# Query and gate projections of a decoder step as 2x2x2 Strassen products

## The reference

```python
# layer 0: HGRN2 mixer, then a ConvFFN; then ONE set of keys and values for layer 1
hn = rmsnorm(h, kv_norm)
k, v, fl = jnp.split(hn @ w_kvf, [D_MODEL, 2 * D_MODEL], axis=-1)
k = rmsnorm(k.reshape(B, T, FOX_HEADS, FOX_HEAD_DIM), k_norm)
logf = jax.nn.log_sigmoid((fl + b_f).astype(jnp.float32))
# layer 1: forgetting attention
hn = rmsnorm(h, norm_mix[layer])
qg = hn @ fox_w_qg[j]                                # 1024 -> 2048
q, gate = jnp.split(qg, 2, axis=-1)
q = rmsnorm(q.reshape(B, T, FOX_HEADS, FOX_HEAD_DIM), q_norm[j])
o = fox_attention(q, k, v, cumulative logf)          # prompt: causal; samples: 512 cached keys and values each
mix = (o.reshape(B, T, D_MODEL) * jax.nn.sigmoid(gate)) @ fox_w_o[j]
h = h + mix                                          # then a second ConvFFN
```

## Time and profile before

| | us |
|---|---|
| median of three runs | 1550.22 |
| lowest, highest | 1549.51, 1550.86 |
| the profiled execution | 1551.19 |
| its span | 1549.6 |
| PE busy in the span | 1524.7 (98%) |
| PE weight loads | 1447.2 (93%) |
| DVE, ACT, POOL busy | 955.0, 747.9, 455.9 |

### The profile page before, as it was taken

The page is one execution under the profiler, slowest core; times in us unless marked ns, Lnnn a source line. Parts: engine busy times, 40 slices in busy tenths (PEclk is TensorE's granted clock), DMA queues, the critical chain, the costliest instruction groups (busy, mean ns, idle before and its releaser), DMA issues. The chain is left out here.

```text
span 1549.6 us, 36591 instructions
## 1 busy us (share of the span) xinstructions
PE 1524.7 (98%) x13662; PEld 1447.2 (93%) x13662; DVE 955.0 (62%) x1699; ACT 747.9 (48%) x1283; POOL 455.9 (29%) x500
## 2 busy tenths in 40 slices
PE   7999999999999999999999999999999999999999
PEld 7999999989999999999999999755899999999999
DVE  5777777767877676533344444688539876767222
ACT  6444444435466566422344455666435565666111
POOL 1222222224575554000010000222126665551000
PEclk9999999999999999999999999999999999999999
DMA  6222222213132222223233334599422222213321
GB/s 217 69 86 93 91 85 78 78 69 113 61 126 91 95 94 92 81 76 89 89 126 116 128 97 150 182 345 367 142 87 82 100 91 94 95 62 118 104 90 46
DMA packets 53363, 174.22 MB, mean 112 GB/s; under 512 B 7298, under 2 KB 9746, under 8 KB 53250
## 3 DMA queue, kind: packets, MB, share of 16 engines
q1 hardware_dynamic: 48578, 156.43, 30.6%
q0 software_dynamic: 4672, 16.24, 2.9%
HBM read 160.07 MB, written 12.57 MB: 111 GB/s over the span
## 5 line engine op out<-in xcount | busy, mean ns | idle before, releaser
L545 ACT ACTIVATE w_hi<-w_raw 128x1024 fp32r<-128x1024 f32 (+1 forms) x143 | 146.9, 1027 | 304.5 <-PE acc L2073 268.6
L1048 DVE TENSOR_TENSOR w_lo<-w_raw,w_hi 128x1024 fp32r<-128x1024 f32 (+1 forms) x141 | 173.4, 1230 | 144.6 <-ACT w_hi L545 142.9
L2073 PE MATMUL acc<-xl,w_hi 128*128 128x288 f32 x1008 | 224.1, 304 | 8.8 <-DVE xl L1060 7.9
L2073 PE MATMUL acc<-xh,w_hi 128*128 128x288 f32 x1008 | 216.1, 296 | 0.0
L2073 PE MATMUL acc<-xh,w_lo 128*128 128x288 f32 x1008 | 215.8, 296 | 0.0
L2073 PEld LDWEIGHTS acc<-xl,w_hi 128*128 128x128 f32 x1008 | 160.9, 189 | 17.0 <-issue 13.2
L2266 PE MATMUL aux<-ffn_xsh,w_lo 128*128 128x288 f32 x576 | 169.9, 295 | 0.0
L2266 PE MATMUL aux<-ffn_xsh,w_hi 128*128 128x288 f32 x576 | 169.7, 295 | 0.0
L2266 PE MATMUL aux<-ffn_xsl,w_hi 128*128 128x288 f32 x576 | 169.3, 294 | 0.2
L2073 PEld LDWEIGHTS acc<-xh,w_hi 128*128 128x128 f32 x1008 | 162.5, 189 | 0.0
L2073 PEld LDWEIGHTS acc<-xh,w_lo 128*128 128x128 f32 x1008 | 162.4, 189 | 0.0
(11 more groups left out here) (347 smaller groups left out, 3445.1 us busy)
## 6 DMA issues: line engine op xcount, KB each, us to landing
w_raw<-w_fi_in SPq DMA_DIRECT2D x88, 512.0 KB, 3.7
w_raw<-w_fo_in SPq DMA_DIRECT2D x32, 512.0 KB, 3.5
att_Vd<-cache_v_in SPq DMA_DIRECT2D x32, 512.0 KB, 5.9
w_raw<-w_mix_in SPq DMA_DIRECT2D x31, 512.0 KB, 3.5
w_raw<-w_kv_in SPq DMA_DIRECT2D x16, 512.0 KB, 3.6
w_raw<-w_qg_in SPq DMA_DIRECT2D x16, 512.0 KB, 3.5
dec_Kd<-cache_k_in SPq DMA_DIRECT2D x16, 512.0 KB, 7.1
w_raw<-cache_k_in SPq DMA_DIRECT2D x16, 512.0 KB, 7.8
```

The lines of the kernel that those rows point to most:

```text
L545: nc.scalar.activation((w_hi[:, pos.slot % SPL] if dst is None else dst)[:, 0:width], w_raw[:, pos.slot, 0:width] if raw is None else raw[ ...
L1048: nc.vector.tensor_tensor(low[:, 0:width], w_raw[:, pos.slot, 0:width] if raw is None else raw[:], high[:, 0:width].bitcast(F32), ALU.subt ...
L2073: mm = nc.tensor.matmul(dst[:, hf, 0:HALF], W[:, 128 * (j0 + j):128 * (j0 + j) + 128], x[:, HALF * hf:HALF * hf + HALF], start=(first and ...
```

## The change

- Query block p and gate block p become one Strassen pair: seven products of 12 matmuls, `q_product`, six in `qg_pair(p)` and the seventh, `q_gate_first(p)`, in the next pair (for the last pair at its end).
- The token-side operands `q_xh`, `q_xl` (7 x 4 tiles of 288) take the place of `x2h`/`x2l`. They are made in KV pairs 2 to 5: `q_operand` (four DVE operations on `h`, now with `rms` and gain in them), `q_operand_sums` (four on POOL), `q_operand_hi` (one ACT copy of 2016 columns) and `q_operand_lo` (one DVE subtraction of 2016).
- The weight sums are made in QG by `q_sum`, `q_sum_hi`, `q_sum_lo`, `q_weight_diff`; the low part of the whole block (`q_block_lo`) and of a gate half (`q_gate_lo`) and the square of the query tile (`q_square`) go to POOL. The sigmoid's last exponential moves out of QG into `att(i)`.
- The sums need room: `h` is written to memory (`h_keep`, 2.36 MB) on SP's queue at the start of KV, ahead of the seven constants, and read back after the last cached values.
- The attention buffers lie elsewhere now, mostly on the operands: SP's `key_bias(0)`, `key_bias(1)`, `key_pages(0)` and `key_pages(1)` wait for products of the last QG pair.
- The key mean of pair 7 goes inside the last value block; the scan over the cached log-forget values is done before KV pair 7.

```diff
             sp.dma_start(pg[:], d["pages"]).then_inc(ld_table, 16)
+            sp.wait_ge(h_ok, 2 * DT)
+            sp.dma_start(d["h_keep"], h[:].rearrange("p m t -> p (m t)")).then_inc(w_half, 16)
             for dst, src in ((w_log[:], d["w_log"]), (group_sum[:], ...
...
-            sp.wait_ge(block_done, B_QG)
+            for p in range(2, DT):
+                for j in range(2):
+                    load(Pos(B_QG + 2 * p + j), d["w_qg"][2 * p + j], ready=(lo_done, B_QG + 2 * p - 2))
+            load(Pos(B_WO1), d["w_o1"][0], ready=(lo_done, B_QG + 14))
+            sp.wait_ge(c_dram, 16)
+            sp.wait_ge(grp_ps, 5 * (FAST + DT - 1) + 1)
             sp.dma_start(tri[:], d["att_masks"][:, 0:P]).then_inc(ld_mask, 16)
-            sp.wait_ge(c_dram, 16)
             key_bias(0, 0)
-            for j in range(4):
-                load(Pos(B_QG + 12 + j), d["w_qg"][12 + j])
+            sp.wait_ge(grp_ps, 5 * (FAST + DT - 1) + 2)
             key_bias(1, 1)
+            sp.wait_ge(grp_ps, 5 * (FAST + DT))
             key_pages(0)
-            load(Pos(B_WO1), d["w_o1"][0])
             key_pages(1)
             sp.wait_ge(block_done, B_WO1)
             sp.wait_ge(cs_dram, 32)
+            sp.wait_ge(km_ps, 16)
             sample_bias(0)
...
+            sp.dma_start(h[:].rearrange("p m t -> p (m t)"), d["h_keep"]).then_inc(w_half, 16)
             sp.wait_ge(d_ps, NSEQ)
...
+            def qg_pair(p):                       # TensorE
+                k, s, tile = p % 2, FAST + p, T_QG + 2 * p
+                x, y, z = [aux[:, b, 0:HALF] for b in (k, 2, 3)]
+                n = q_weight_n(p)
+                pe.wait_ge(lo_done, B_QG + 2 * p + 1)
+                if p == 0:
+                    pe.wait_ge(s_lo, q_part_n(4))
+                    pe.wait_ge(kln_ok, DT)
+                pe.wait_ge(evac, tile - 2)
+                q_product(x, 0, w_hi[:, 0, 0:512], w_lo[:, 0, 0:512], False).then_inc(grp_ps, 1)
+                if p == 0:
+                    last_turn_v()
+                    pe.wait_ge(vt_ok, 14)
+                pe.wait_ge(evac, tile - 1)
+                q_product(y, 1, w_hi[:, 0, 512:1024], w_lo[:, 0, 512:1024], False).then_inc(grp_ps, 1)
+                pe.wait_ge(s_lo, n + 1)
+                q_product(z, 2, q_wxh[:, 0], q_wxl[:, 0], False).then_inc(grp_ps, 1)
+                if p:
+                    if p == 1:
+                        pe.wait_ge(vt_ok, 16)
+                    key_mean(p + 7, acc[:, 1])
+                    q_gate_first(p - 1)
+                if p == DT - 1:
+                    pe.wait_ge(s_lo, n + 3)
+                    score(0, 0)
+                pe.wait_ge(s_lo, n + 2)
+                pe.wait_ge(snap_ok, 3 * s + 1)
+                q_product(x, 3, q_wxh[:, 1], q_wxl[:, 1], True).then_inc(grp_ps, 1)
+                pe.wait_ge(s_lo, n + 3)
+                pe.wait_ge(snap_ok, 3 * s + 2)
+                q_product(z, 4, w_hi[:, 1, 0:512], w_lo[:, 1, 0:512], True).then_inc(block_done, 1)
+                pe.wait_ge(s_lo, n + 4)
+                pe.wait_ge(snap_ok, 3 * s + 3)
+                q_product(x, 5, w_hi[:, 1, 512:1024], w_lo[:, 1, 512:1024], True).then_inc(grp_ps, 1)
+                if p == DT - 1:
+                    q_gate_first(p)
+                    key_mean(15, acc[:, 1])
...
+                if last:                          # DVE, end of its qg_pair(p)
+                    first_probs()
+                else:
+                    q_sum_lo(2, p + 1)
+                if p:
+                    gate_logsig(p - 1)
+                if last:
+                    gate_halves(p)
+                    square_lo(sqq, p + 8)
+                    gate_rest(p)
...
+            def kv_pair(p):                       # ACT
+                if p:
+                    hi(Pos(B_KV + 1 + 2 * p))
+                    if p == 1:
+                        gate_logits()
+                    value_out(p - 1, aux[:, 3, :], aux[:, 2])
+                hi(Pos(B_KV + 2 + 2 * p))
+                act.wait_ge(kr_ok, p + 1)
+                wait(act, kn_ok, p)
+                nc.scalar.activation(sq[:], KT[:, p], ACT.Square).then_inc(ksq_ok, 1)
+                square_hi(p)
+                mean_root(p, aux[:, 0:2])
+                if 2 <= p < 6:
+                    q_operand_hi(p - 2)
```

More of the change, by code:

```diff
@@ L960, in first_ex @@
                 ex(0, 0, 1)
-            qg_pair(0, 6, 3, 4)
-            qg_pair(1, 7, 3, 4, True, first_ex)
+            for p in range(DT):
+                qg_pair(p)
             def att(i):
@@ L1620, in _, with gate_halves @@
             dve.wait_ge(wg_ok, 2)
-            def qg_pair(k, p, i, step, last=None):
-                b = B_QG + 2 * p
-                if isinstance(p, int) and p == 0:
-                    lo(Pos(B_QG + 1))
-                    dve.wait_ge(c_dram, 16)
+            kv_pair(DT - 1)
+            q_sum_lo(0, 0)
+            q_sum(2, 0)
+            q_sum_lo(1, 0)
+            q_sum_lo(2, 0)
+            def gate_halves(p):
+                k, s = p % 2, FAST + p
+                dve.wait_ge(grp_ps, 5 * s + 5)
+                dve.wait_ge(snap_ok, 3 * s + 2)
+                nc.vector.tensor_tensor(GT[:, p, HALF:T], aux[:, k, 0:HALF], snap5, ALU.add).then_inc(gt2_ok, 1)
@@ L1638, in qg_pair @@
-                nc.vector.sem_inc(evac, 1)
-                if last is None:
-                    lo(Pos(B_QG + 3 + 2 * k, i, step))
-                    key_gain(QT, p, p + 8, gq[:, 0:1])
-                    gate_logsig(p)
+                    mx(0, 0, 0)
+                    mx(0, 0, 1)
+                if p:
+                    key_gain(QT, p - 1, p + 7, gq[:, 0:1])
+                if not last:
+                    q_sum_lo(1, p + 1)
+                dve.wait_ge(block_done, B_QG + 2 * p + 1)
@@ L1682, in first_max @@
                 scale_p(0, 0, 1)
-            qg_pair(0, 6, 3, 4)
-            qg_pair(1, 7, 3, 4, first_max)
+            for p in range(DT):
+                qg_pair(p)
             def att(i):
@@ L2367, in kv_pair @@
                     turn_v(1 - k, p - 1)
-                gemm(Pos(B_KV + 1 + 2 * k, i, step), T_KV + 1 + 2 * p, (T_KV + 1) % 2, range(DT), xh, xl)
+                gemm(Pos(B_KV + 1 + 2 * k, i, step), T_KV + 1 + 2 * p, (T_KV + 1) % 2, range(DT), xh, xl,
+                     mid={5: lambda: key_mean(p, aux)} if final else None)
                 if first:
@@ L2377, in _ @@
             kv_pair(1, 1, 0, 4)
-            with pe.Fori(1, 4) as i:
+            with pe.Fori(1, 3) as i:
                 kv_pair(0, 2 * i, i, 4)
                 kv_pair(1, 2 * i + 1, i, 4)
-            def qg_pair(k, p, i, step, mid=None):
-                first = isinstance(p, int) and p == 0
-                gemm(Pos(B_QG + 2 * k, i, step), T_QG + 2 * p, T_QG % 2, range(DT), x2h, x2l, wait_x=(x_lo, 24) if first else None)
-                if first:
-                    turn_v(1, 7)
-                gemm(Pos(B_QG + 1 + 2 * k, i, step), T_QG + 1 + 2 * p, (T_QG + 1) % 2, range(DT), x2h, x2l,
-                     mid={5: lambda: key_mean(p + 8, sqq)} | (mid or {}))
@@ L2389, in _, with q_product @@
-            qg_pair(0, 0, 0, 4)
-            qg_pair(1, 1, 0, 4)
-            with pe.Fori(1, 3) as i:
-                qg_pair(0, 2 * i, i, 4)
-                qg_pair(1, 2 * i + 1, i, 4)
+            kv_pair(0, 6, 3, 4)
+            kv_pair(1, 7, 3, 4, True)
+            def q_product(dst, o, wh, wl, add):
+                for j in range(4):
+                    c = slice(P * j, P * j + P)
+                    for n, (W, X) in enumerate(((wh, q_xl), (wl, q_xh), (wh, q_xh))):
+                        mm = nc.tensor.matmul(dst, W[:, c], X[:, o, j], start=(not add and j == 0 and n == 0), stop=(j == 3 and n == 2),
+                                              skip_group_check=True)
+                return mm
@@ new lines, in q_gate_first, with last_turn_v @@
+            def q_gate_first(p):
+                pe.wait_ge(lo_done, B_QG + 2 * p + 2)
+                pe.wait_ge(gt2_ok, FAST + p + 1)
+                q_product(aux[:, p % 2, 0:HALF], 6, q_gate_w[p % 2][0], q_gate_w[p % 2][1], True).then_inc(block_done, 1)
+            def last_turn_v():
+                pe.wait_ge(v2_ok, DT)
+                for c in range(NCH):
+                    nc.tensor.transpose(acc[:, 1, 0, CH * c:CH * c + CH], vT2[:, 1, CH * c:CH * c + CH], ident[:])
+                nc.tensor.transpose(acc[0:NS, 1, 1, 0:P], vT2[:, 1, SEQ:T], ident[:]).then_inc(v2_ps, 1)
@@ L2509, in att @@
                 turns(i, 2)
-            qg_pair(0, 6, 3, 4)
-            qg_pair(1, 7, 3, 4, {2: first_score})
+            for p in range(DT):
+                qg_pair(p)
             for i in range(NSEQ):
```

515 lines of the change are left out of this document (347 added, 168 removed).

## The result

The changed kernel takes 1558.76 us (median of 6 runs, 1557.78 to 1560.88), the kernel before 1550.36 beside it (6 runs): a ratio of 1.0056, interval 1.0043 to 1.0069. I had forecast 1545.0 with a range up to 1551.5. The sign was wrong too. The profiled execution has a span of 1558.3 us against 1549.6.

A forecast was written before the change was run, and what follows sets the result against it. TensorE was taken to bound QG, so removed matmuls count in full. -12.7 + 2.7 + 1.2 + 2.3 + 1.1 = -5.4 us, from 1550.22 to 1544.8, rounded to 1545.0; range 1539.5 to 1551.5.

The forecast's parts named there:

- Matmuls removed, -12.7: In QG, 84 matmuls for 96 in each of 8 pairs, 96 fewer at 0.1319 us: -12.7 us, the most possible.
- Inside QG, 0: In QG's pairs, ACT, DVE and POOL all stay under 11.6 us a pair, so no loss: 0, up to 8 us.
- Its start, 0: At QG's start, key mean and weight sums are ready in time: 0, bounds 0 to 1 us.
- End of QG, +2.3: In the last QG pair, TensorE waits for DVE's `gate_halves(7)` before the seventh product: +2.3 us, bounds 0.5 and 4.
- Operands in KV, +1.2: In KV pairs 2 to 5, making the operands delays the next value block's low part 0.3 a pair: +1.2 us, 0 to 3.
- The spill, +2.7: At KV's start, the 2.36 MB write of `h` delays the constants from 768.2 to 770.9: +2.7 us, upper bound +5.5.
- rival 1: TensorE's clock falls at KV's start, losing 3.4 us: 1548.4; with a second fall at QG's end, 1550. Chance 0.22.
- a sign of being wrong: At KV's start: the forecast is wrong if the clock falls at 770; it was to stay at 1.00.
- the lower bound of 0: At KV's start, the spill costs 0 if the constants pass the big write; struck because they can't pass.
- The start of attention, +1.1: At attention's start, a late own mask makes POOL's mask and DVE's maximum 2.4 us late, half hidden: +1.1 us, 0 to 3.
- 4.2 MB flow from 16.5: Both samples' keys flow from 16.5 us after the last QG pair's start and end near 28, at 362 GB/s.
- Rival 3: Transfers bind attention: 4.2 MB moved out of QG bring 11.6 us back, +5 in sum, 1555. Chance 0.13.

The follow-up runs named there:

- Run 6: Changed kernel with the three mends of run 5, and each page of the first sample's keys issued after its own last-pair product: 1545.44 us, ratio 0.9974.
- Run 10: Run 6 with ACT's first snapshot of pair 0 and DVE's fourth low part moved earlier at the start of QG: 1543.99 us, ratio 0.9957.
- run 3: Changed kernel with the spill of `h` issued behind the seven loads of constants: 1553.69 us, ratio 1.0020.
- run 5: Changed kernel with three mends together, those of run 1, run 3 and run 4: 1549.69 us, ratio 0.9996.
- run 1: Changed kernel with sample 0's bias and the own mask issued between the first and second sample's keys: 1554.78 us, ratio 1.0028.
- run 2: Changed kernel with POOL's `own_mask(0)` one place later, behind `mask(1,0)`: 1556.47 us, ratio 1.0042.
- run 4: Changed kernel with DVE's `gate_halves(7)` ahead of the scalings of head pair 0's probabilities: 1560.61 us, ratio 1.0068.
- Run 9: Changed kernel with odd samples' keys on their own semaphore, so the second sample's keys don't wait for the first's landing: 1556.47 us, ratio 1.0037.
- Run 8: Kernel before, with `h` also written to memory ahead of the seven constants at the start of KV: 1555.54 us, ratio 1.0037.

## Why the prediction was wrong, by its own steps

**Matmuls removed, -12.7: right in size.** 13566 matmuls against 13662 are 96 fewer, the interval is 11.6 us, and QG's clean part shows it. Run 6's QG is 107.12 against 114.71, with 3.5 us of idle TensorE in it: 11.1 us won without them. The last 1.6 us I can't name from these rows.

**Inside QG, 0: right. Its start, 0: wrong by 1.56** (1.08 and 0.48 us in pair 0). I had looked at what was ready, not at ACT's and DVE's order there. Run 10 took back 1.2.

**End of QG, +2.3: right as a wait, 2.46 us with DVE's `gate_halves(7)` as its releaser.** Beside it stand 0.70 us before the first score and a clock fall that begins at 982.2 and costs 1.4 up to the first transposes (none of that in the term).

**Operands in KV, +1.2: nothing.** With the spill behind the constants KV takes 108.42 to 108.46, against 108.48 (runs 3, 5, 6).

**The spill, +2.7: the step whose direction was right and whose price was 6.6** in this trace, and 5.2 to 6.7 over the five traces with the write ahead (changed, 1, 2, 4, 9). The constants were ready 3.4 us later (forecast 2.7), and TensorE idle for 3.6 more. The rest is the clock: 2.7 of rival 1's 3.4 us, to which I had given a chance of 0.22, and whose fall at 770 I had named as a sign of being wrong. Run 8 shows both parts on the kernel before, run 3 shows that nothing else is in it.

The write itself landed as forecast, 8.0 us after its issue, at 769.5 (forecast 769.4). What held up the last constant was mostly its issue: SP issued it at 768.78 against 765.54 before, and from there it took 2.8 us against 2.6. SP was late because its issues behind the write took longer, a term that my sum didn't have.

The Trainium skill, "DMA: Bandwidth & Descriptors", section "Queues, rings and completion order", had served to strike the lower bound of 0. My "can't pass" was more than it says: it gives the order in which descriptors are consumed, and adds that a later one may finish its write before an earlier one. The trace agrees with the order, since `w_log`, issued 0.4 us behind the write, took 7.4 us to land instead of 3.2, and the seven loads landed 3.3 to 4.8 us later than before.

**The start of attention, +1.1: the step that failed.** Attention is 7.5 us longer. I had named the chain rightly, own mask, POOL's list, maximum. But I let "4.2 MB flow from 16.5" where SP waits in `key_pages(1)` for the first sample's keys: the own mask was in use 17.4 us after the first transposes, not 12.4. Run 9, which has the flow that I laid out, comes to 13.1. Counted to the second head pair's scores, it is 2.0 us behind the kernel before and the changed kernel 6.3. So the step failed mainly by a wait on SP that I passed over: 4.3 us. The rest of my term was too small but of the right kind: in run 9 the maximum came 14.3 us after the transposes, against 11.1 before, so 3.2 us late instead of 2.4, and cost 2.0 instead of 1.1. Another 1.2 us come behind these scores. The clock is at its lower level there until 1009.5, with TensorE at work for 3.2 us of it, which would be 1.6 by my estimate; neither the term nor rival 1 had a fall at this place.

**Rival 3, transfers bind attention: wrong for the changed kernel, where the values weren't waited for, and right one layer down.** As soon as the mask's stall was gone (runs 1, 5, 6), TensorE waited for values.

The sum by stages, in the traces: KV +6.6, QG -5.5, attention +7.5 make +8.6, against +8.7 in the span. The first two alone would have made this execution 1.2 us slower: of 12.7 us won in QG, 6.1 were lost in it to four small waits and a clock fall, and 1.1 I can't name.

## What to carry to other kernels

When an edit moves a transfer later, walk its queue instruction by instruction and write down each wait on the issuing engine, including those that never waited before. A wait that was satisfied long ahead is invisible in the old profile. Put small loads that gate a chain (a mask, constants) ahead of large ones and ahead of any wait in the list; in both places of this case that was worth 4 to 5 us. Time won ahead of a stage that its transfers bind is given back in it, in part or whole, until these start earlier too (runs 4, 5 and 6). And before a difference of 1 to 2 us between two traces is put down to an edit, look at the granted clock of their other executions.

## What the hardware did that I had not expected

**The clock's fall after a wait is not the same each time, even for the same code.** After waits of 3.54 to 4.33 us ahead of the logits the clock was at its lower level for 6.8 us in the traces of the changed kernel and runs 1 and 2, and for 3.4 in those of runs 4 and 9, which have the same code up to there. Runs 5 and 6 have the same waits of 0.64, 0.61 and 2.13 us around the first transposes of attention; in run 5's trace the clock is down from 981 to 989, in run 6's it never falls. Among the executions of run 6 the mean granted clock is 0.998 to 1.000, in run 5 0.997 to 0.999, so neither trace stands for its kernel.

The Trainium skill, "TensorE: Matmul & The Clock Gate", section "HAM oscillation — how this bites in real kernels", tells of such cold starts behind waits for transfers. Here the traces agree for the changed kernel and run 8, and run 6 shows that a wait of 2.13 us, for DVE, may also pass without one.

**SP's issues take longer behind a large write.** The four constants issued first behind the 2.36 MB write took 1.26 to 1.76 us each on SP; in run 3, ahead of it, three of these four took 0.36 to 0.49 and one 1.23. What held SP no run shows.

**An operation of DVE beside one of POOL can take almost four times as long.** The low part of 512 columns whose two inputs both lie in SBUF (`qgw_Sw` and `w_hi`) took 2.60 to 2.70 us on DVE in seven of the eight pairs. Each time it started just behind POOL's low part of 1024 columns; in pair 0 it ran from 890.78, while POOL's ran from 890.47 to 892.86. In the eighth pair it started ahead of POOL's (968.86 against 969.91) and took 0.68. The 24 low parts of this size that read one input from PSUM took 0.67 to 0.69, one of them (888.66) also beside a low part of POOL's (887.66 to 888.94). I had counted 0.69 for all four. A pair still takes 11.6 us, but the wait of 0.48 us in pair 0 ends with this operation; in run 10 it starts at 882.01 there, ahead of POOL's at 883.54, and takes 0.68.
